# Two layers on one core: 44 instead of 40 first keys read densely, 12 first-table panels moved among the gate products, a one-hot ring of two groups, second-table gathers six steps behind

## What is computed

```python
def peer(xn, w_query, sub_keys_1, sub_keys_2, expert_u, expert_v):
    # 256 tokens, 8 heads, 128 x 128 experts, 16 picked for each token and head
    q = (xt @ w_query).reshape(t, PEER_HEADS, PEER_QUERY_DIM)
    s1, s2 = q1 . sub_keys_1, q2 . sub_keys_2          # 128 scores each
    v1, i1 = lax.top_k(s1, 16); v2, i2 = lax.top_k(s2, 16)
    top_s, top_pos = lax.top_k(v1[..., :, None] + v2[..., None, :], 16)
    expert_idx = i1 * 128 + i2                          # of the 16 best pairs
    gates = softmax(top_s)
    a = einsum('thkd,td->thk', expert_u[expert_idx], x)
    hid = gelu(a) * gates
    out = einsum('thk,thkd->td', hid, expert_v[expert_idx])
```

## Time and profile before

| | us |
|---|---|
| median of 3 runs | 3002.77 (2999.91 to 3003.15) |
| the profiled execution's own time | 3000.82 |
| its span in the trace | 2998.8 |
| mean granted PE clock | 0.943 of full |
| busy: PE / DVE / ACT / POOL | 2758.8 / 1923.8 / 1178.2 / 652.6 |
| steps of the last layer | from 1852 to the end |

### The profile page before, as it was taken

One profiled execution on the slowest core, in us unless ns is written; L12 is line 12 of the kernel. 1 busy time (PEld: TensorE's weight loads), 2 busy tenths in 40 slices (PEclk: granted clock), 3 DMA queues, 4 the chain that ended last, 5 costly groups with the idle time before them and its releaser, 6 DMA issues.

```text
span 2998.8 us, 45605 instructions
## 1 busy us (share of the span) xinstructions
PE 2758.8 (92%) x17100; PEld 2069.8 (69%) x17100; DVE 1923.8 (64%) x3184; ACT 1178.2 (39%) x2298; POOL 652.6 (22%) x568
## 2 busy tenths in 40 slices
PE   8999999999999997999999999999977887887884
PEld 7886788888888887989999889777754432222230
DVE  6888566556656565455444558987869875555555
ACT  1003443333334344435334444655556542222223
POOL 0000000000000000040000002444447664444453
PEclk9999999999999998999999999999977678998996
DMA  6333545555555553443455657999999999999998
GB/s 244 141 141 106 206 161 187 184 194 182 191 187 187 190 184 129 155 155 141 177 186 184 239 200 259 363 418 409 416 383 396 390 416 417 415 413 394 414 407 319
DMA packets 131299, 785.52 MB, mean 262 GB/s; under 512 B 34631, under 2 KB 34631, under 8 KB 35847
## 3 DMA queue, kind: packets, MB, share of 16 engines
q1 hardware_dynamic: 55424, 393.68, 35.6%
q0 software_dynamic: 75712, 389.74, 32.3%
HBM read 940.23 MB, written 4.19 MB: 315 GB/s over the span
## 4 chain that ended last, share of the span: by engine, by line
PE 57%; DMA 19%; DVE 12%; issue 7%; ACT 3%; POOL 2%; DVEq 1%; POOLq 0%; SPq 0%; ACTq 0%
DMA s_u<-in_expert_u,s_u_index 15%; PE bank L1847 10%; PE bank L1841 10%; PE bank L1842 10%; PE bank L1843 10%; PE bank L1848 5%; PE bank L1937 4%; PE bank L2240 4%; DVE s_u L1706 4%; DMA s_v<-in_expert_v,s_v_index 3%; PE bank L2291 2%; POOL s_u L585 2%; DVE s_cacc L1217 2%; DVE s_w_lo L1128 1%; DVE s_yrow L1390 1%
## 5 line engine op out<-in xcount | busy, mean ns | idle before, releaser
L1128 DVE TENSOR_TENSOR s_w_lo<-s_raw,s_w_hi 128x2048 fp32r<-128x2048 f32 x258 | 592.6, 2297 | 578.0 <-ACT s_w_hi L628 577.6
L628 ACT ACTIVATE s_w_hi<-s_raw 128x2048 fp32r<-128x2048 f32 x256 | 490.4, 1916 | 751.7 <-PE bank L1843 476.3
L1847 PE MATMUL bank<-s_a,s_w_hi 128*128 128x512 f32 x1408 | 493.8, 394 | 3.4 <-DVE s_w_lo L1128 3.2
L1706 DVE CUSTOM_DVE_ANT_0 s_u<-s_u,s_xn_late 128x1024 f32<-128x1024 f32 x256 | 303.7, 1224 | 244.0 <-DMA s_u<-in_expert_u,s_u_index 217.1
L2291 PE MATMUL bank<-s_v,s_spread 128*32 128x512 f32 x2048 | 310.3, 715 | 152.0 <-DMA s_v<-in_expert_v,s_v_index 121.6
L1050 ACT ACTIVATE s_spread<-s_ident,s_hid 32x32 f32<-32x32 f32 x1024 | 325.7, 318 | 205.0 <-DVE s_hid L1756 175.8
L1848 PE MATMUL bank<-s_a,s_w_lo 128*128 128x256 f32 x1408 | 394.8, 280 | 0.0
L585 POOL DMA_INDIRECT s_u<-in_expert_u,s_u_index x256 | 292.5, 1142 | 432.1 <-DVE s_halfdot L1706 267.9
L601 POOL DMA_INDIRECT s_v<-in_expert_v,s_v_index x256 | 309.9, 1211 | 191.7 <-PE bank L2291 109.6
L1706 DVE CUSTOM_DVE_ANT_0 s_u<-s_u,s_xn 128x1024 f32<-128x1024 f32 x256 | 303.8, 1224 | 56.0 <-DMA s_u<-in_expert_u,s_u_index 49.6
L1841 PE MATMUL bank<-s_a,s_w_hi 128*128 128x256 f32 x1152 | 325.3, 282 | 4.1 <-DVE s_a L1152 2.4
(11 more groups left out here) (321 smaller groups left out, 3821.8 us busy)
## 6 DMA issues: line engine op xcount, KB each, us to landing
s_raw<-in_stream SPq DMA_DIRECT2D x292, 1024.0 KB, 4.7
s_raw<-in_expert_v SPq DMA_DIRECT2D x40, 1024.0 KB
s_raw<-in_dense_u SPq DMA_DIRECT2D x37, 1024.0 KB
s_u<-in_expert_u,s_u_index POOLq DMA_INDIRECT x256
s_v<-in_expert_v,s_v_index POOLq DMA_INDIRECT x256
s_panel_early<-in_dense_u POOLq DMA_DIRECT2D x3, 1024.0 KB, 11.4
s_xres<-in_x SPq DMA_DIRECT2D x2, 1024.0 KB, 5.9
out<-s_out_row SPq DMA_DIRECT2D x32, 64.0 KB
```

What stands on the lines that cost most here:

```text
L628: act.activation(w_hi[s % 2][:, :], raw[s][:, :], ACT.Copy).then_inc(hi_ready, 1)
L1128: dve.tensor_tensor(w_lo[s % 2][:, :], raw[s][:, :], w_hi[s % 2][:, :].bitcast(f32), ALU.subtract)\
L1706: ins = dve.tensor_tensor_reduce(out=u_slot[k % NU][:, half], in0=u_slot[k % NU][:, half], in1=xn_late[:, half] if t else xn[:, 0, half], ...
L1847: pe.matmul(dst, left[0], both, start=start, stop=False)
```

## The change

- `DENSE` is 44: 44 panels of each table, and only picks with a first key below 84 are gathered.
- 32 first-table panels (`FIRST_U`) stay in steps 0 to 16, evenly spread; the other 12 (`LATE_U`) go one by one into steps 18 to 29, in banks 4 and 5. Gates of tokens whose late panel is still missing are copied into `ha` and multiplied by the panel's gelu afterwards (`landed`).
- The ring of one-hot groups from ACT has two groups instead of four, which makes room for the larger `ha`.
- All fours of a step stand behind the adds, in steps 18 and 19 too.
- `LAG` is 6.
- 44 second-table panels are spread over the same steps 34 to 60.
- The two key searches of a route are interleaved in its first quarter (`best_keys_of_both`), pairs and experts move one quarter forward.

```diff
-DENSE = 40
+DENSE = 44
+FIRST_U, LATE_U = 32, 12
@@
 def u_panels_in(i):
-    if i < 2:
-        return range(3 * i, 3 * i + 3)
-    return range(6 + 34 * (i - 2) // 15, 6 + 34 * (i - 1) // 15) if i < 17 else range(0)
+    if i < 17:
+        return range(FIRST_U * i // 17, FIRST_U * (i + 1) // 17)
+    return range(FIRST_U + LATE_U * (i - 17) // 13, FIRST_U + LATE_U * (i - 16) // 13) if i < 30 else range(0)
+def gated_before(g):
+    fours = 8 * (g - 18) if g < 20 else 4 * (g - 16)
+    return max(0, min(fours, T // 4) // 2 - 2)
+LANDS_IN = {d: i + 2 for i in range(30) for d in u_panels_in(i) if d >= FIRST_U}
@@
-    return range(3 * (i - 34) // 2, min(DENSE, 3 * (i - 33) // 2)) if i >= 34 and 3 * (i - 34) // 2 < DENSE else range(0)
+    return range(DENSE * (i - 34) // 27, DENSE * (i - 33) // 27) if 34 <= i < 61 else range(0)
@@
-    NU, NV, NW, NH, BATCH, LAG = 5, 7, 4, 4, 4, 4
+    NU, NV, NW, NH, BATCH, LAG = 5, 7, 4, 4, 4, 6
@@ one_keys (ACT)
-                wait(act, one_key_used, f - 7)
+                wait(act, one_key_used, f - 3)
@@ dense_hidden (ACT)
+                if late >= 0:
+                    done = GATE_TOKENS * gated_before(LANDS_IN[d])
+                    if late == 0:
+                        act.wait_ge(expert_ready, TT * PH)
+                    wait(act, late_landed, late - 1)
+                    act.activation(late_act[:, late % 2, 0:done], bank[b][:, 0:done], ACT.Gelu_apprx_tanh)
+                act.activation(ha[:, dense_block(d), done:], bank[b][:, done:T], ACT.Gelu_apprx_tanh).then_inc(bank_empty[b], 1)
@@ gated (DVE)
+                if missing:
+                    dve.tensor_copy(some[:, 0:missing, :], gates[:, 0:missing, :])
+                dve.tensor_tensor(some[:, missing:, :], some[:, missing:, :], gates[:, missing:, :], ALU.mult).then_inc(bank_empty[b], 1)
+            def landed(d):
+                late, (b, k) = d - FIRST_U, u_bank(d)
+                groups = gated_before(LANDS_IN[d])
+                for group in (groups - 2, groups - 1):
+                    gates_taken = n.after(f"empty{6 + group % 2}", FIRST_U // 4 + 2 + group // 2)
+                    dve.wait_ge(bank_empty[6 + group % 2], gates_taken)
+                dve.wait_ge(bank_empty[b], n.after(f"empty{b}", k + 1))
+                some = ha[:, dense_block(d), 0:GATE_TOKENS * groups]
+                dve.tensor_tensor(some, some, late_act[:, late % 2, 0:GATE_TOKENS * groups], ALU.mult).then_inc(late_landed, 1)
@@ PE, step i
-                for f in token_fours_in(i)[:-4]:
-                    token_four(f)
@@
-                for f in token_fours_in(i)[-4:]:
+                for f in token_fours_in(i):
                     token_four(f)
```

More of the change, by code:

```diff
@@ L1082, in one_keys @@
                 act.activation(four, four, ACT.Relu, scale=-1.0, bias=1.0).then_inc(one_key_ready, 1)
-            slots_stored = [n.after(f"empty{6 + t}", DENSE // 4 + 1) for t in range(TT)]
+            slots_stored = [n.after(f"empty{6 + t}", FIRST_U // 4 + 1) for t in range(TT)]
             for g in range(ROUTES * GROUPS):
@@ L1723, in one_keys_2 @@
                     for t in range(TT):
[L1724 removed]
+                        dve.wait_ge(bank_empty[6 + t], n.after(f"empty{6 + t}", FIRST_U // 4 + 1))
                 wait(dve, one_key_used, 2 * (m - 2))
@@ L1806, in _ @@
                         route(route_in(g), turn)
-                    fours = token_fours_in(g)
+                    for d in range(FIRST_U, DENSE):
+                        if turn == 0 and LANDS_IN[d] == g:
+                            landed(d)
+                    fours, missing = token_fours_in(g), sum(LANDS_IN[d] > g for d in range(FIRST_U, DENSE))
                     for f in fours[turn * len(fours) // 4:(turn + 1) * len(fours) // 4]:
                         if f >= 4 and f % 2 == 0:
-                            gated(f // 2 - 2)
+                            gated(f // 2 - 2, missing)
                         if f % 2 == 0:
```

76 lines of the change are left out of this document (50 added, 26 removed).

## The result

The changed kernel takes 3027.6 us (median of 6 runs, 3021.7 to 3030.5) against 3001.8 of the kernel before: a ratio of 1.0085, 95% interval 1.0074 to 1.0096. The forecast was 2993, range 2975 to 3014. The profiled execution took 3024.4 us, its span is 3022.3, 23.5 us longer than that of before.

The account below looks back on a forecast made before the run. The prediction took DMA to bound the last layer, DVE its beginning. Terms -14 - 3.5 + 6.5 + 3 - 2 = -10 against the profiled 3000.82 gave 2990.8; with 1.95 for the median, 2993 us, range 2975 to 3014.

Parts of the forecast that it names:

- the 2.8 MB that it didn't count: First 80 us, where DMA is not the bound: gathers lose 1.2 MB, panels worth 1.6 MB load later.
- The bytes: Last layer: gathers lose 17.2 MB, panels add 8.4; 6.0 MB net counted at 415 GB/s, -14 us.
- The routes: Four route steps ahead of 1934, where DVE is the bound: interleaved key searches save 0.8 us a route, -3.5 us.
- Steps 18 and 19: Gate products wait for fours behind adds and late gathers: 63 us for both steps, 16.5 us idle DMA, +6.5 us.
- Steps 20 to 31: Gate steps: bounds of 14 to 16 us leave no slack, 16.8 us a step, 8 us idle DMA, +3 us.
- the second rival: Gate steps: landings of 12 us or more make the step 19 us, +26, 3019; 19% together with rival 1.
- rival 1: Gate steps: PE at mean clock 0.75, 19.6 us a step, +34, 3027; 19% together with the second rival.
- gathers held back by PE's adds: Steps 32 to the end: LAG 6 takes this wait away, -2 us of at most 9.
- The end: Behind the last gather's issue: a rest of queued rows remains whatever the order, so no change.
- The signs that were named: Lead of some 25 us, step 18 wait about 15, steps 18 and 19 60 or more, gate steps 16 to 17.5.

Follow-up runs that it names:

- a_lag4: The changed kernel with LAG 4 instead of 6, nothing else: 3002.2 us, 1.0001 of the kernel before.
- b_lag6: The kernel before with LAG 6 alone: 3024.6 us, 1.0076 of the kernel before.
- b_keys: The kernel before with the interleaved key search alone, pairs and experts one quarter earlier: 3001.1 us, 0.9998 of the kernel before.
- a_light: The changed kernel without 15 of the 16 matmuls of each of the 12 late first-table panels: 3031.6 us, 1.0101 of the kernel before.

## Why the prediction was wrong, step by step

Time is DMA's busy time and its idle time, so the misses can be read in one table. Busy and idle are summed from the packet records; the forecast column is the prediction's, with the 2.8 MB that it didn't count booked as idle at the start. A packet that straddles a cut can move a term by 0.3 us.

| last layer, us | forecast | changed | a_lag4 |
|---|---|---|---|
| DMA busy (before 1120.8) | -21 | -5.5 | -10.3 |
| idle up to group 17 (before 7.6) | +3.5 | +7.2 | +4.8 |
| idle in 18 and 19 (5.2) | +6.5 | +10.2 | +2.6 |
| idle in 20 to 31 (0.5) | +3 | +10.9 | +0.9 |
| idle in 32 to 63 (3.1) | -2 | -1.0 | +0.4 |
| idle behind it (9.7) | 0 | +1.5 | 0 |
| sum | -10 | +23.5 | -1.5 |

By the medians the miss is 34.6 us. 25.4 of them go with LAG alone; the 8.5 us between the first and the last column are the bytes (10.7 us less of busy time saved than forecast), with smaller terms of both signs. The larger failure is that of LAG, the loop over the late gather, told at steps 20 to 31.

- **The bytes.** The counts were right to 0.1 MB, the time was not: 13.9 us of less work for four keys instead of 21. With the idle time that comes with them they are worth 7 to 8 us (6.7 and 8.3). The Trainium skill (page "DMA: Bandwidth & Descriptors", section "Anatomy of one DMA — SWDGE (gpsimd) path") gives a DMA issued from GpSimd a fixed part of about 2.0 us; carried over to the eight more loads, which SyncE issues, that is an estimate of 16 us, and 21 - 16 = 5. That came nearer than my rows, but the records show no fixed part: the mean 8 KB packet of the panels' queue took 313.4 ns with 40 keys and 316.7 with 44, which is 2.2 us over 10,880 packets. What failed here is the assumption that a price per MB, taken from the mean, is what a MB less gives back: the slow packets in that mean don't go away with the bytes, and a skipped row still leaves a small packet.
- **The routes.** Sized well in the sum (in b_keys 4 us up to group 3, forecast 3.5; 1.4 instead of 0.8 us off a route step of the changed kernel), and booked wrongly: b_keys shows that time won while DVE sets the pace is taken back as soon as DMA does. The prediction had seen this for panels and not for its own saving.
- **Steps 18 and 19.** The mechanism happened as told. DVE and PE of the changed kernel, timelines:

```profile
2204.13 0.26 DVE L1799 COPY s_ha<-bank 128x96 f32<-128x96 f32 x1 [11.72 <-PE bank L2344]
...
2229.46 0.26 DVE L1799 COPY s_ha<-bank 128x96 f32<-128x96 f32 x1 [7.10 <-PE bank L2344]
```

```profile
2190.16 7.85 PE L2304 MATMUL bank<-s_xnt,s_raw 128*128 128x256 f32 x32
2201.02 1.07 PE L2355 MATMUL bank<-s_v,s_spread 128*32 128x512 f32 x8 [0.30 <-DMA s_v<-in_expert_v,s_v_index]
2202.01 1.98 PE L2344 MATMUL bank<-s_one_key,s_one_key 128*128 128x44 f32 x16
```

  The gate product comes 19.8 us behind `s_hid` (forecast 28, before 13), with waits of 11.7 us (forecast 15) and 7.1; 54 us instead of 63, and 15.4 us of idle DMA instead of 16.5. The landing was 14 instead of 21 us (25 in b_lag6). The prediction also had the first bytes 3 us behind an issue; behind first-table gather 84 of the changed kernel, issued at 2235.61 when its queue had just run dry, they came after 1.7 us. What the sum got wrong is the base: before, DMA is idle 5.2 us here, not 10, so the term was +10.2 and not +6.5. It was read from GB/s, in which slow packets look like idle time; the DMA share in the row of before says it, 43.85 x (1 - 0.88) = 5.3.
- **Steps 20 to 31: the step that failed.** The prediction took 16.8 us a step, from "a stalled DVE issues nothing, so the queue gets short by itself" and "At 8 to 9 us the step is 16"; 17.6 us a step came. The idle base was wrong too, 0.5 us before and not 5. The late gathers 79, 83, ... 127 took 7.7 to 19.5 us to land, 12.8 in the mean (issue to last semaphore increment, 13 gathers), 11.7 in the kernel before and 10.4 in b_lag6; in a_lag4 it is even 14.7, and the steps are short all the same (16.4), so it is the distance in the queue that counts. A stall does shorten the landing, but not to 8 or 9: the nine late gathers with a wait of POOL of over 4 us among their last eight issues took 11.5 us in the mean, the other four 15.8. After a stall POOL issues eight gathers in a row and the late one is the last of them; that it lands late because of its own burst is a reading, not varied by itself.
- **The length of the loop.** The loop had been found and priced in the second rival, as landing plus 7 us: 19 us a step at a landing of 12. By that rule 12.8 and 10.4 us give 19.8 and 17.4; 17.6 and 15.7 (b_lag6) came, 2 us less, because the loop closes over two steps. Two steps are issue 2.7, landing, 5 to 6 us to the gate product, and DVE's own 13.5 to the next `s_hid` but one, that is (2.7 + 12.8 + 5 + 13.5) / 2 = 17.0 and in b_lag6 (2.7 + 10.4 + 5.7 + 13.3) / 2 = 16.1, as estimates from these rows. b_lag6 shows the period of two: its gate product waits 3.5, 4.2, 4.8 and 5.8 us in steps 22, 24, 26 and 28, and not in 23, 25 and 27. So the rival's price was too high and its chance, 19% with rival 1, was far too small for the nearest row, 10.3 us, of a kernel with fewer bytes.
- **The forecast's lengths and its sum don't agree.** `s_hid` of group 17 at 2208 - 25 = 2183, 63 us and 12 steps of 16.8 us put `s_hid` of group 31 at 2448, 23 us behind that of before (2425). From there on only some 4 MB fewer are moved (227.6 against 223.5 MB in a_lag4), 10 us, and 2 us were hoped for: +11 in all, some 3013, and not -10. The lengths were nearer the mark (group 31 came at 2450.0); adding them up beside the terms would have shown 20 us that one of the two had wrong, 9 of them the idle bases (10 and 5 instead of 5.2 and 0.5).
- **Rival 1 gave 3027, the measured number, and is wrong.** The clock was 0.84 in the gates and a step 17.6 us, not 0.75 and 19.6; a_light, with less PE work, is no faster, and LAG alone takes the time away. Its number was right by luck.
- **LAG 6 was not priced as a change of its own.** Its parts stood in other terms, and the gain at which it was aimed ("gathers held back by PE's adds", -2 us) is not there: steps 32 to 63 take 554.8 us with LAG 6 and 554.1 with LAG 4.
- **The end.** That the last part is "there whatever the order" fell: 17.4 us with LAG 6, 14.1 with LAG 4, 16.9 against 14.2 in the kernel before.
- **The signs that were named.** The lead at group 17 came (23.8 us, forecast 25), and so did the wait in step 18 (11.7 us, forecast 15), but steps 18 and 19 took 54 and not 60 us or more. The gate steps (17.6 us, clock 0.84) were just above the 16 to 17.5 us named as right and still below the 18 named as wrong: that sign was set too wide, since 0.8 us a step is 10 us. DMA's share behind step 32 is 1.00, and no wait for `xn_late` shows, as forecast.

Two things stay open: why slow packets grow in number when bytes go (below), and what turns the sign of the order of the fours, which the rows point to but no run varied by itself.

## What to carry to other kernels

When an edit moves a transfer later in its queue, follow it to the instruction that waits for it last, and see whether that instruction lets the transfer itself be issued: such a loop costs its landing time under load in every round, and a round may be more than one step, so count which issue really stands behind the wait. Change the distance by itself, in both kernels, before sizing anything else; here it was 25 of 26 us. Add a forecast up twice, by stages and by terms. And time saved where another resource will be the bound a moment later was worth nothing here (b_keys).
